# A two-layer decoder trunk: pairs, loads and products of w_mod moved by a section or more

## What is computed

```python
for layer in range(DEPTH):
    mod = c_act @ w_mod[layer] + b_mod[layer]
    shift, scale, gate = jnp.split(mod, 3, axis=-1)
    hdn = rms_norm(x, norm_w[layer]) * (1.0 + scale[:, None, :]) + shift[:, None, :]
    q1, k1, v1, g1, q2, k2, v2, g2 = jnp.split(hdn @ w_in[layer], 8, axis=-1)
    if layer % 2 == 0:      # differential attention (A), dilated window attention (B)
        y1 = diff_attention(q1, k1, v1, ...)
        y2 = dilated_attention(q2, k2, v2, ...)
    else:                   # MoBA (C; one block here, so causal), stick-breaking (D)
        y1 = moba_attention(q1, k1, v1, ...)
        y2 = stick_breaking_attention(q2, k2, v2)
    y = jnp.concatenate([y1 * jax.nn.silu(g1), y2 * jax.nn.silu(g2)], axis=-1) @ w_out[layer]
    x = x + gate[:, None, :] * y
```

## Time and profile before

| | |
|---|---|
| median of 3 runs | 338.74 us (338.22 to 339.8) |
| the profiled execution | 338.16 us, of which the span is 336.4 |
| PE busy | 303.1 us (90%) |
| DVE busy | 234.1 us (70%) |
| ACT busy | 196.3 us (58%) |
| POOL busy | 13.2 us (4%) |
| DMA | 70.31 MB, mean 209 GB/s |
| chain that ended last | PE 66%, DVE 12%, ACT 9%, DMA 8% |

### The profile page before, as it was taken

How to read it: one execution, slowest core, us unless ns; L and a number is a source line. 1 busy time by engine, 2 the same in 40 slices (tenths; PEclk the granted TensorE clock), 3 DMA queues, 4 the chain that set the end, 5 groups by cost and what they waited for, 6 DMA issues and landing times.

```text
span 336.4 us, 4790 instructions
## 1 busy us (share of the span) xinstructions
PE 303.1 (90%) x1709; PEld 239.4 (71%) x1709; DVE 234.1 (70%) x482; ACT 196.3 (58%) x399; POOL 13.2 (4%) x20
## 2 busy tenths in 40 slices
PE   2498988999989599996999999999999999988895
PEld 2487766776555468883565888889888789887684
DVE  3899998879783865567867647879774535469533
ACT  4524487555565836993534454675654886997400
POOL 0000000000005323000000000000000000000000
PEclk9999999999999979997999999999999999999999
DMA  6999998573687484089982505587556146000011
GB/s 254 373 417 406 406 406 330 186 242 104 228 306 267 162 322 187 2 274 415 320 278 94 179 5 187 187 311 241 205 185 253 64 152 222 27 36 2 0 64 62
DMA packets 19879, 70.31 MB, mean 209 GB/s; under 512 B 2192, under 2 KB 2576, under 8 KB 19856
## 3 DMA queue, kind: packets, MB, share of 16 engines
q1 hardware_dynamic: 19856, 70.01, 57.4%
HBM read 68.95 MB, written 1.05 MB: 208 GB/s over the span
## 4 chain that ended last, share of the span: by engine, by line
PE 66%; DVE 12%; ACT 9%; DMA 8%; issue 3%; SPq 1%; ACTq 0%; DVEq 0%
PE proj L1075 45%; PE score L1075 12%; DMA raw<-in_w 6%; PE mixed L1075 4%; DVE w_lo L746 3%; DVE raw L766 2%; DMA raw<-in_w_mod 2%; PE turned L1120 2%; PE turned L1102 2%; ACT w_hi L476 2%; DVE probs L1019 1%; ACT logits L687 1%; ACT logits L685 1%; ACT logits L683 1%; DVE xs L961 1%
## 5 line engine op out<-in xcount | busy, mean ns | idle before, releaser
L746 DVE TENSOR_TENSOR w_lo<-raw,w_hi 128x1024 fp32r<-128x1024 f32 x68 | 82.4, 1221 | 16.6 <-ACT w_hi L476 16.2
L476 ACT ACTIVATE w_hi<-raw 128x1024 fp32r<-128x1024 f32 x68 | 70.8, 1051 | 20.6 <-DMA raw<-in_w 19.5
L1075 PE MATMUL proj<-w_hi,hy_hi 128*128 128x512 f32 x144 | 60.5, 420 | 9.7 <-DVE hy_lo L800 5.1
L766 DVE CUSTOM_DVE_ANT_0 raw<-raw,c_rows 128x1024 f32<-128x1024 f32 x48 | 57.8, 1222 | 4.5 <-DMA raw<-in_w_mod 4.5
L1075 PE MATMUL proj<-w_hi,hy_lo 128*128 128x512 f32 x144 | 57.4, 398 | 0.0
L1075 PE MATMUL proj<-w_lo,hy_hi 128*128 128x512 f32 x144 | 57.1, 397 | 0.0
L1075 PE MATMUL proj<-hy_hi,w_hi 128*128 128x256 f32 x176 | 52.5, 298 | 0.0
L1075 PE MATMUL proj<-hy_lo,w_hi 128*128 128x256 f32 x176 | 49.7, 282 | 0.0
L1075 PE MATMUL proj<-hy_hi,w_lo 128*128 128x256 f32 x176 | 49.7, 282 | 0.0
L1075 PEld LDWEIGHTS proj<-w_hi,hy_hi 128*128 128x128 f32 x144 | 27.7, 192 | 18.1 <-DVE hy_lo L951 5.8
L1075 PEld LDWEIGHTS proj<-hy_hi,w_hi 128*128 128x128 f32 x176 | 33.5, 191 | 2.1 <-issue 2.1
(11 more groups left out here) (144 smaller groups left out, 428.0 us busy)
## 6 DMA issues: line engine op xcount, KB each, us to landing
raw<-in_w SPq DMA_DIRECT2D x76, 512.0 KB, 4.8
raw<-in_w_mod SPq DMA_DIRECT2D x48, 512.0 KB, 6.1
xs<-in_x SPq DMA_DIRECT2D x1, 1024.0 KB, 5.3
qT<-in_w SPq DMA_DIRECT2D x2, 512.0 KB, 4.0
kT<-in_w SPq DMA_DIRECT2D x2, 512.0 KB, 6.4
out_x<-xs SPq DMA_DIRECT2D x4, 256.0 KB, 2.0
cst<-in_constants SPq DMA_DIRECT2D x1, 520.0 KB, 6.3
logits<-in_a_lambda SPq DMA_DIRECT2D x1, 128.0 KB, 11.8
```

Of the source, the lines that this page charges most:

```text
L476: nc.scalar.activation(w_hi[:, slot(n), :, :], raw_tile(("w", n)), ACT.Copy).then_inc(hi_done, 1)
L746: nc.vector.tensor_tensor(w_lo[:, slot(n), :, :], raw_tile(("w", n)), w_hi[:, slot(n), :, :], ALU.subtract).then_inc(lo_done, 1)
L766: nc.vector.tensor_tensor_reduce(out=tile, in0=tile, in1=c_rows[:, :], scale=1.0, scalar=0.0, op0=ALU.mult, op1=ALU.add, accum_out=col(V_M ...
L1075: return nc.tensor.matmul(o, a, b, start=start, stop=stop, skip_group_check=True)
```

## The change

- Pairs 4 to 7 begin one section sooner (45, 49, 53, 57). Pair 4 keeps its mix in section 53, the other three are mixed one section sooner.
- The held pieces leave SyncE's list and stand at the end of GpSimd's program, behind the same wait for section 59.
- `MOD_AT` gives the products of w_mod 17 to 39 other sections, and `EARLY` puts the high parts of pieces 28 to 35 one to three sections later. The list of loads is sorted by the same rule, so its order changes from load 40 on.
- GpSimd begins the first two biases after the turn of Q2's first half and waits for the second half only ahead of the third.
- At the start the two diagonals are made by ScalarE instead of VectorE.

```diff
-EARLY = {24: 14, 27: 16, 28: 14, 29: 13, 30: 12, 31: 11, 32: 15, 33: 14, 35: 14, 36: 10}
+EARLY = {24: 14, 27: 16, 28: 13, 29: 12, 30: 10, 31: 9, 32: 12, 33: 11, 35: 12, 36: 10}
...
-PAIR_AT = [27 + 4 * j for j in range(4)] + [46 + 4 * j for j in range(4)] + [STEPS + 23 + 4 * j for j in range(4)]
+PAIR_AT = [27 + 4 * j for j in range(4)] + [45 + 4 * j for j in range(4)] + [STEPS + 23 + 4 * j for j in range(4)]
...
-MOD_AT = [25 + 2 * i for i in range(24)] + [STEPS + 16 + 3 * i for i in range(8)]
+MOD_AT = [25, 26, 28, 29, 30, 33, 35, 37, 38, 41, 42, 43, 45, 48, 49, 51, 52, 55, 57, 59, 61, 63, 66, 68] + [STEPS + 16 + 3 * i for i in range(8)]
...
 def pv_lag(j):
-    return 6 if group(j) == 0 else 7
+
+    return 6 if group(j) == 0 else 8 if j == 4 else 7
...
-        later.sort()
-        loads += [key for _, _, key in later]
-
-        behind_held = next(key for at, _, key in later if at > HELD_FROM)
+        loads += [key for _, _, key in sorted(later)]
...
             for i, key in enumerate(loads):
-                if key == behind_held:
-
-                    wait_step(sp, HELD_FROM)
-                    for n, b in zip(HELD, held):
-                        sp.dma_start(b, w[n].rearrange("p (k n) -> p k n", k=2)).then_inc(held_in[HELD.index(n)], 16)
...
             rms_seed(x_ms[:, 0:2], x_y[:, 0:2], x_t[:, 0:2], x_ln, x_seed, x_seed2, 1)
+            act.wait_ge(x_rms, 1)
+            for t in range(2):
+                nc.scalar.activation(x_diag[:, t, :], ident, ACT.Copy, scale=x_t[:, t:t + 1]).then_inc(diag_ok, 1)
             first_blocks(0)
...
             refine(x_ms[:, 0:2], x_y[:, 0:2], x_t[:, 0:2]).then_inc(x_rms, 1)
-            dve.wait_ge(x_rms, 1)
-            for t in range(2):
-                x_diagonal(t)
             first_blocks(0)
...
             pool.wait_ge(cst_in, 16)
-            wait_turned(pool, ("qk", 0, Q2, 1))
             for M in range(8, 16):
+                if M in (8, 10):
+
+                    wait_turned(pool, ("qk", 0, Q2, (M - 8) // 2))
                 if M >= 12:
                     pool.wait_ge(logit_ok, M - 3)
...
                 nc.gpsimd.tensor_tensor(b, b, dilated, ALU.add).then_inc(bias_ok, 1)
+
+
+            wait_step(pool, HELD_FROM)
+            for i, n in enumerate(HELD):
+                nc.gpsimd.dma_start(held[i], w[n].rearrange("p (k n) -> p k n", k=2)).then_inc(held_in[i], 16)
```

## The result

The changed kernel takes 328.61 us (median of 4 runs, 328.3 to 329.23) against 339.27 for the kernel before on the same chips: ratio 0.9687, 95% interval 0.9648 to 0.9726, so 2.7 to 3.5% faster. The forecast was 328.4. Of all the executions behind this document three took far longer, 383, 601.5 and 1669 us, and the medians, ranges and ratios leave them out. The profiled execution took 328.47 us, its span 326.7, which is 9.7 less than before.

A forecast was written before the change was run, and what follows sets the result against it. TensorE, busy 303.1 of 336.4 us, was taken as the bound, with only idle and slow time to win. Terms summed to -10.05: 328.1 from the profiled 338.16, 328.7 by the median, stated as 328.4, range 325.2 to 333.4.

The forecast's parts named there:

- Piece 25's stall: Before section 50: TensorE's wait for this weight tile goes whole, 4.77 idle and 1.74 of slow clock, 6.5 us saved.
- Product 34's stall: Before section 65: its load no longer waits for section 59, so 2.96 idle and 1.53 slow go, 4.5 us saved.
- Held pieces on GpSimd: Four loads behind the wait for section 59: issue at most 1.70 us each, covered by 12 us, price 0.
- The doubled turn: Section 53: pair 5's first turn behind the second subln turn shares the `turned` bank, TensorE waits for ScalarE's copy, +0.7 us.
- ScalarE becomes late: Sections 53 to 62: TensorE waits for its copies, +0.95 us at pair 6's second turn, +0.75 at pair 7's.
- Rival 1: ScalarE keeps up: VectorE reaches pair 5's logits 2.4 us sooner, the three new waits vanish, 326.0 us; chance 0.15.
- Product 39 off the chain: Section 71: it leaves the chain between the two updates of x, removing TensorE's idle before x's turn, -0.85 us.
- Rival 2: Sections 58 and 62: ScalarE's lag grows to 2 us or more and costs clock as well, 331.5 us; chance 0.18.
- Rival 3: A stall survives: loads freed of section 59 come no sooner, only piece 25's stall goes, 332.9 us; chance 0.08.
- rival 4: Section 66: held pieces come late on GpSimd, TensorE idles 12 us and loses clock, 341.6 us; chance 0.04.

## Why the prediction was right, point by point

- *Piece 25's stall, -6.5.* Right. No gap and full clock in 112 to 120. The run with the held pieces alone keeps the stall (4.71 us), the one with all other parts has lost it. SyncE issues the load at 105.61, where I had counted section 45's end as 105.8. What I had not seen is how much hangs on the new EARLY: without it, in the run with the products alone and in the one with the old EARLY, piece 25 or 26 is late by 1.5 to 3.3 us. Whether the products' new sections are needed as well is not shown. By the rule that sorts the loads, the new EARLY alone would put piece 25 behind piece 22 in the ring just the same (load 59 behind load 52), and that kernel was not run.
- *Product 34's stall, -4.5.* Right. Alone it gave 4.8 us; undone in the changed kernel it cost 5.4. It is the queue's order, as the earlier trace rows said. One reading was off: section 59 freed SyncE at 143.46 and not at 145.50; the two us between went into issuing the four held loads, at 0.33 to 0.44 us each.
- *Held pieces on GpSimd, 0.* Right. Four issues in 2.3 us, 0.53 to 0.73 each, against my bound of 1.70, and no wait for a held piece. They took 3.7 to 8.5 us to land, not my 3.31; the last lay there by 150.7 and is first used at 158.1. The Trainium skill's warning (SBUF — State Buffer, "Who interferes with whom") that GpSimd is locked out beside a copy-like instruction of VectorE is not seen here, and not refuted: beside the four issues VectorE ran a low part and a product of w_mod, which are no copies.
- *The doubled turn, +0.7.* It measured 0.87, the nearest row's value; my discount was wrong.
- *ScalarE becomes late, +0.95 and +0.75.* Right in place and cause, low in size: 1.28 and 1.09, and 0.34 at the first subln turn, for which I had no term. Timeline of ACT in the changed kernel, against my starts of 118.3, 128.4, 136.9 and 145.4:

```profile
118.33 0.40 ACT L572 ACTIVATE probs<-logits,stat 128x128 f32<-128x128 f32 x1 [2.78 <-DVE stat L844]
...
128.92 0.47 ACT L539 ACTIVATE probsT<-turned 128x384 f32<-128x384 f32 x1
...
131.99 1.04 ACT L469 ACTIVATE w_hi<-raw 128x1024 fp32r<-128x1024 f32 x1
...
137.43 0.48 ACT L539 ACTIVATE probsT<-turned 128x384 f32<-128x384 f32 x1
...
138.88 1.04 ACT L469 ACTIVATE w_hi<-raw 128x1024 fp32r<-128x1024 f32 x1
...
146.09 0.47 ACT L539 ACTIVATE probsT<-turned 128x384 f32<-128x384 f32 x1
```

  The two intervals, 8.51 from copy to copy and 8.66, answer my 8.5 and 8.5. The late half microsecond comes at the doubled turn: up to 126.81 ScalarE waits 1.22 us for TensorE in three pieces, where I had 0.7. One sentence of my account fell: I hung the lag on pair 5's logits, late by VectorE's list. The run with the products sooner shows that this is not what sets it. So the start at 118.33, which my list hit, did not matter, and that part of the account was right by luck. Rival 1 was wrong in its condition too: with those logits a microsecond sooner ScalarE did not keep up.
- *Product 39 off the chain, -0.85.* Right: the gap before x's turn is gone, also in each run with the new sections of the products.
- *Rival 2* did not come: waits of 1.28 and 1.09, 2.37 us together, left the clock up. *Rival 3* and *rival 4* are out by the windows and GpSimd's rows.

The sum by the measured terms: the new waits are 3.58 where I had 2.4, 1.2 us more. What was removed up to x's first turn comes to 13.0 (the 9.4 by which TensorE reaches that turn sooner, counted from section 43, plus the 3.58), where my rows gave 12.45. Another 0.3 lies before and behind. The span moved by 9.7, where I had 10.05. Every term of the sum had its cause right, except for what starts ScalarE's list; that the forecast came so near is in part luck, since a 1.2 too small on one side met 0.8 too small on the other.

## What to carry to other kernels

When one queue issues every load in order, a wait in it for one late buffer is charged to all loads behind it: look in the queue's own waits, and give that load another queue, if its slower issue still leaves the data in time (here 0.53 to 0.73 us an issue, with some 7 us to spare). When a large stall of the main engine goes, count the next engine's list of work between two of its hand-overs: it was hidden in the stall's time. Where that list has no wait in it, each instruction costs in full what it takes, as two high parts of 0.94 us did; the third, which stood ahead of a wait, cost next to nothing. And undo each part of a bundle once: here the edit that gave the change its name cost 1.9 us, hidden by the others' gain.

## What the runs showed of the hardware

The length of an idle of TensorE did not tell what clock followed. After 2.96 us and after 3.12 the clock fell to its lower level, 1.2 GHz, but after 3.27, in the run with the old EARLY, it stayed at 2.4. At the start an idle of 2.58 was followed by the lower level in the changed kernel's trace, and one of 2.59 by the upper in the run with the diagonals back. And a like idle cost 1.5 us of slow clock before and 2.8 with the held pieces on SyncE. My estimate from these runs: a forecast that removes such an idle should give its clock part as a range of 0 to 3 us.

GpSimd and VectorE slow each other in small amounts: in the changed kernel a low part of VectorE took 1.57 us at 120.30, beside a GpSimd instruction, against the usual 1.22; and a GpSimd addition took 1.70 at 107.69, beside a low part, against 0.73 at 103.16, where VectorE idled.
